# Modulation rows of a two-block network from four standing columns, two products per weight slice, folded afterwards

## The chip, the cores and the metric

The kernel runs on one core of a Trainium2 chip. The metric is the device time in microseconds (us) of the whole program; lower is better. Besides plain executions there is one profiled execution of the kernel before, and all durations below come from it.

## What is computed

The reference chains two networks of two layers each over 512 tokens of width 1024, all in float32. The part that the change touches is the modulation of the second network. Once per layer two vectors (one for the main tokens, one for the context tokens) are multiplied by a 1024 x 6144 matrix, a bias is added, and the two results are cut into six vectors of 1024 each: shift, scale and gate for the mixer, shift, scale and gate for the feed-forward part.

```python
silu_c = jax.nn.silu(c)
silu_cc = jax.nn.silu(c_ctx)
for i in range(DEPTH):                      # DEPTH = 2
    mod = (silu_c @ ada_w[i] + ada_b[i])[:, None, :]
    mod_c = (silu_cc @ ada_w[i] + ada_b[i])[None, None, :]
    sh_m, sc_m, g_m, sh_f, sc_f, g_f = jnp.split(mod, 6, axis=-1)
    shc_m, scc_m, gc_m, shc_f, scc_f, gc_f = jnp.split(mod_c, 6, axis=-1)
    h = modulate(rmsnorm(x, norm_mix_w[i]), sh_m, sc_m)
    ...
    x = x + g_m * y
    x = x + g_f * swiglu(modulate(rmsnorm(x, norm_ffn_w[i]), sh_f, sc_f), ...)
```

## The kernel before

The program is a chain of stages written by hand, each a block with a part for SyncE (SP, which issues the DMAs), ScalarE (ACT), VectorE (DVE) and TensorE (PE). The engines meet only at semaphores. A stage that begins with `join` waits on every engine for the last signals of the stage before, and also for the DMAs that the stage before registered with `loading`: those are waited for by each engine that joins.

Float32 precision in the large products comes from splitting both operands in two. A weight chunk of 1 MB (four slices of 128 x 512 floats) lands in one of the slots, ACT casts it to `w_hi` in two halves (`hi_until`, L244), DVE subtracts to get `w_lo` in two halves (`lo_until`, L254), and PE makes three products for each 128-row slice (`split_products`, L289 to L291): hi by hi, lo by hi, hi by lo. `w_hi` and `w_lo` have two buffers each, so the cast of chunk c waits until PE is done with chunk c-2 (`chunk_used`). In this stage the raw chunks have four slots, two in `raw` and two at the end of `arena`; SP issues the load of chunk c+4 when DVE has finished `w_lo` of chunk c (`stream`, L227).

`modulation` (L1467) has 24 chunks: twelve groups `g` of 512 output columns, with two chunks each. The stationary operand of PE is `pair`, the silu of the two vectors in hi and lo form, two columns each; the weights are the moving operand. After each group DVE adds the bias and writes two rows (`rows`, L1535). At the end SP stores both rows to `mod_rows` in DRAM (L1490), whose gate parts are broadcast back much later by `gate_tables`; PE turns the rows by 48 small transposes (L1523) into columns, DVE copies them to `modT` (L1538) and folds the norm weights in (L1543). The next stage, `mod_norm`, starts with a join on ACT (L465 in the first layer, L468 in the second). The last `hi_until` and `lo_until` also split the first chunk of that next stage, chunk number 24 counted from 0, before the last bias addition.

The two instances of the stage are called layer 0 and layer 1 below.

Of the kernel before, what the change touches and what calls it, by code (L numbers as in the profile page):

```python
# [19 lines left out]
F32 = mybir.dt.float32  # L20
F32R = mybir.dt.float32r
I32 = mybir.dt.int32
ALU = mybir.AluOpType
# [3 lines left out]
P = 128  # L27
D = 1024
# [14 lines left out]
KQ = 4  # L43
BANK = 512
# [76 lines left out]
def column_plan():  # L121

    names = [("mix_g0", 8), ("mix_g1", 8), ("xa_g0", 8), ("xa_g1", 8), ("mem_g0", 8), ("mem_g1", 8),
             ("ffn_g0", 8), ("ffn_g1", 8), ("ret_g", 4), ("hg_g", 4), ("lb", 12), ("odq", 1), ("odk", 1),
             ("xaq0", 2), ("xaq1", 2), ("xak0", 2), ("xak1", 2), ("cw0", 66), ("cw1", 66), ("cb0", 22),
             ("cb1", 22), ("nm0", 8), ("nm1", 8), ("nf0", 8), ("nf1", 8), ("c", 8), ("cc", 8),
             ("sgun", 4), ("decb", 4), ("ghn", 1)]
    plan, at = {}, 0
    for name, n in names:
        plan[name] = (at, n)  # L130
        at += n
    return plan, at


class Kernel:


    def __init__(self, nc, ctx, ins, out):
# [12 lines left out]
        self.w_lo = sb("w_lo", [P, 2, SLOT], F32R)  # L151
        self.arena = sb("arena", [P, ARENA])
        self.plan, ncol = column_plan()
        self.cols = sb("cols", [P, ncol])
        self.perms = sb("perms_sb", [P, 3 * P])
# [23 lines left out]
    def col(self, name, i=0, n=1):  # L179
        a = self.plan[name][0] + i  # L180
        return self.cols[:, a:a + n]
# [105 lines left out]
def split_products(pe, out, w, x, first, last):  # L287

    pe.matmul(out, w[0], x[0], start=first, stop=False)  # L289
    pe.matmul(out, w[0], x[1], start=False, stop=False)  # L290
    return pe.matmul(out, w[1], x[0], start=False, stop=last)  # L291
# [18 lines left out]
def stage_sems(k, stage, *names):  # L310

    k.entry = dict(k.latest)
    k.loads, k.begun = [x for x in k.loads if len(x[1]) < 4] + k.begun, []
    out = []
    for name in names:
        engine, what = name.split(":")
        key = f"{stage}_{what}" if engine == "dma" else f"{engine}_{what}"
        if key not in k.signals:
            k.signals[key] = Signal(k, engine, k.nc.alloc_semaphore(key))
        k.signals[key].base = k.signals[key].total  # L320
        out.append(k.signals[key])
    return out
# [1143 lines left out]

def modulation(k, W, l):  # L1467


    A = Arena(k)  # L1470
    rows, bias = A(6 * D), A(6 * D)
    sc = A(KD, 2)
    first = W[f"ada{l}"]
    n, nk = 6 * D // BANK, KD // KQ
    pair = [x[:, :, 0:2] for x in (k.hi, k.lo)]
    s_c_hi, s_c_lo, s_silu, s_bias, s_side, s_mm_done, s_freed, s_turned, s_modT, s_stored = stage_sems(k, f"ada{l}", "act:c_hi", "dve:c_lo", "act:silu", "dma:bias", "dma:side", "pe:mm_done", "dve:freed", "pe:turned", "dve:modT", "dma:stored")
    block = k.block
    for i in range(n * nk):
        k.chunk_used[first + i] = s_mm_done(i + 1)

    @block.sync
    def _(sp):
        k.join(sp, "pe", "dve", "act", "pool")
        b = k.ins["ada_b_2"]
        sp.dma_start(bias[0:2, :], bass.AP(b.tensor, b.offset + l * 6 * D, [[0, 2], [1, 6 * D]])).then_inc(*s_bias.up(16))
        if l == 0:
            sp.dma_start(k.X[:, TX:TALL, :], k.ins["ctx_2"][0].rearrange("(t p) d -> p t d", p=P)).then_inc(*s_side.up(16))
        k.stream(sp, first + n * nk)
        sp.wait_ge(*s_freed(n))
        sp.dma_start(k.mod_rows, rows[0:2, :]).then_inc(*s_stored.up(16))  # L1490
        k.loading(s_stored(16))
        sp.wait_ge(*s_stored(16))
        if l == 0:
            k.loading(s_side(16))

    @block.scalar
    def _(act):
        k.join(act, "pe", "dve", "act", "pool")
        for i, name in enumerate(("c", "cc")):
            act.activation(sc[:, :, i], k.col(name, 0, 8), ACT.Silu).then_inc(*s_silu.up(1))  # L1500
        act.wait_ge(*s_silu(2))
        act.copy(pair[0], sc).then_inc(*s_c_hi.up(1))
        for i in range(n * nk + 1):
            k.hi_until(act, first + i + 1)

    @block.tensor
    def _(pe):
        k.join(pe, "pe", "dve", "act", "pool")
        pe.wait_ge(*s_c_lo(1))
        for g in range(n):  # L1510
            if g >= 4:
                pe.wait_ge(*s_freed(g - 3))
            for q in range(nk):
                k.wait_split(pe, first + nk * g + q)
                w = k.split_chunk(first + nk * g + q)
                for kk in range(KQ):
                    ins = split_products(pe, k.ps[0:2, g % 4, :], [x[:, q * KQ + kk, :] for x in pair],
                                         [x[:, kk, :] for x in w], q == 0 and kk == 0,
                                         q == nk - 1 and kk == KQ - 1)
                ins.then_inc(*s_mm_done.up(1))  # L1520
        pe.wait_ge(*s_freed(n))
        for i in range(48):
            ins = pe.transpose(k.ps[:, 4, 2 * i:2 * i + 2], rows[0:2, i * P:(i + 1) * P], k.ident[0:2, 0:2])  # L1523
        ins.then_inc(*s_turned.up(1))

    @block.vector
    def _(dve):
        dve.wait_ge(*s_c_hi(1))
        dve.tensor_tensor(pair[1], sc, pair[0].bitcast(F32), ALU.subtract).then_inc(*s_c_lo.up(1))
        k.lo_until(dve, first + 2)  # L1530
        dve.wait_ge(*s_bias(16))
        for g in range(n):
            k.lo_until(dve, first + min(nk * g + 4, nk * n + 1))
            dve.wait_ge(*s_mm_done(nk * (g + 1)))
            dve.tensor_tensor(rows[0:2, g * BANK:(g + 1) * BANK], k.ps[0:2, g % 4, :],  # L1535
                              bias[0:2, g * BANK:(g + 1) * BANK], ALU.add).then_inc(*s_freed.up(1))
        dve.wait_ge(*s_turned(1))
        dve.tensor_copy(k.modT[:].rearrange("p a b -> p (a b)"), k.ps[:, 4, 0:96]).then_inc(*s_modT.up(1))  # L1538
        dve.wait_ge(*s_modT(1))
        for base, name in ((8, f"nm{l}"), (32, f"nf{l}")):  # L1540
            for i in range(2):
                m = k.modT[:, base:base + 8, i]
                dve.scalar_tensor_tensor(m, m, 1.0, k.col(name, 0, 8), ALU.add, ALU.mult).then_inc(*s_modT.up(1))  # L1543
        dve.wait_ge(*s_modT(5))


def mod_norm(k, name, tiles, which, end):
# [119 lines left out]

def ab_mixer(k, W):
    modulation(k, W, 0)
    mod_norm(k, "ab_norm", list(range(TALL)), 0, W["ab_u"])  # L1670
    A = Arena(k)
# [285 lines left out]

def cd_mixer(k, W):
    modulation(k, W, 1)
    mod_norm(k, "cd_norm", list(range(TALL)), 0, W["cd_f"])  # L1960
    A = Arena(k)
# [161 lines left out]
def pack_columns(inputs):  # L2123

    col = lambda a: np.ascontiguousarray(a, dtype=a.dtype).reshape(-1, P).T
    src = {"ret_g": inputs["ev_ret_norm_g"], "hg_g": inputs["ev_hg_norm_g"], "lb": inputs["hg_lb_logits"],
           "odq": inputs["od_q_norm_g"], "odk": inputs["od_k_norm_g"], "c": inputs["c_2"],
           "cc": inputs["c_ctx_2"], "sgun": inputs["ab_sgu_norm_w_2"], "ghn": inputs["cd_head_norm_w_2"],
           "decb": np.concatenate([inputs["cd_decay_b_fwd_2"], inputs["cd_decay_b_bwd_2"]], 1)}
    for l in range(2):  # L2130
        for name, key in (("mix_g", "mix_norm_g"), ("xa_g", "xa_norm_g"), ("mem_g", "xa_mem_norm_g"),
                          ("ffn_g", "ffn_norm_g"), ("xaq", "xa_q_norm_g"), ("xak", "xa_k_norm_g"),
                          ("cw", "ffn_conv_w"), ("cb", "ffn_conv_b"), ("nm", "norm_mix_w_2"),
                          ("nf", "norm_ffn_w_2")):
            src[f"{name}{l}"] = inputs[key][l]
    plan, n = column_plan()
    return np.concatenate([col(np.asarray(src[name])) for name in plan], 1)

# [38 lines left out]
```

## Time and profile before

| | value |
|---|---|
| median of 3 runs (lowest to highest) | 4140.07 us (4135.92 to 4140.22) |
| the profiled execution, its own time | 4140.34 us |
| its span in the trace | 4138.6 us |
| busy share PE, DVE, ACT, POOL | 86%, 42%, 30%, 1% |
| mean granted TensorE clock, share of full | 0.916 |
| modulation of layer 0 in the trace | from 2111.5 to about 2202.8 us |
| modulation of layer 1 in the trace | from 3269.9 to about 3356.6 us |

The busy shares are means over the whole program. The two modulation stages take some 178 us of it together, so a change inside them is read from those two stretches alone.

### The profile page before, as it was taken

The page shows a single profiled execution, that of the slowest core. Times are in us where ns is not written, and L with a number is a line of the kernel's source. Part 1 is how long each engine was busy: PE and PEld are TensorE (multiplying, and loading weights), DVE is VectorE, ACT ScalarE, POOL GpSimd, SP SyncE. Part 2 cuts the span into 40 slices and gives each one's busy share as a digit, 9 for nine tenths or more (in the row PEclk, how much of TensorE's full clock was granted, in tenths as well). Part 3 has the DMA queues.
Part 4 walks back from the last instruction along what each step waited for, and adds up shares of the span by engine and source line. Part 5 has one row for each costly group of instructions (what it writes and reads, how often), then busy time and mean ns, then how long its engine had stood idle before and what let it go on. Part 6 is the DMA issues. An engine that isn't in the chain of part 4 may idle for free. (4 is left out here: it accounts for less than half of the span.)

```text
span 4138.6 us, 39286 instructions
## 1 busy us (share of the span) xinstructions
PE 3546.6 (86%) x16452; PEld 2818.0 (68%) x16452; DVE 1747.7 (42%) x2354; ACT 1225.1 (30%) x1664; POOL 54.2 (1%) x40
## 2 busy tenths in 40 slices
PE   7786696899987787899988978799999889678998
PEld 5464585787874575688746856688878547467876
DVE  2447445444434535444454156431123561433234
ACT  3110243323333333322343124221122341223222
POOL 0003100000000000000000000000000000000000
PEclk9885798999998898999999989899999999679999
DMA  4120130232221022233263120222212441012322
GB/s 141 36 72 0 41 113 20 82 101 83 92 95 61 11 81 72 62 94 100 87 219 108 61 36 1 61 59 64 62 62 67 159 154 64 11 56 77 98 91 82
DMA packets 326817, 313.82 MB, mean 76 GB/s; under 512 B 22304, under 2 KB 250016, under 8 KB 326376
## 3 DMA queue, kind: packets, MB, share of 16 engines
q1 hardware_dynamic: 326640, 311.30, 24.2%
q8 instruction: 131, 2.15, 0.2%
q14 instruction: 46, 0.38, 0.0%
HBM read 309.06 MB, written 2.22 MB: 75 GB/s over the span
## 5 line engine op out<-in xcount | busy, mean ns | idle before, releaser
L289 PE MATMUL ps<-hT_hi,w_hi 128*128 128x512 f32 (+1 forms) x2640 | 968.0, 367 | 25.7 <-DVE arena L829 11.0
L290 PE MATMUL ps<-hT_lo,w_hi 128*128 128x512 f32 (+1 forms) x2640 | 965.9, 366 | 0.0
L291 PE MATMUL ps<-hT_hi,w_lo 128*128 128x512 f32 (+1 forms) x2640 | 965.1, 366 | 0.0
L254 DVE TENSOR_TENSOR w_lo<-raw,w_hi 128x1024 fp32r<-128x1024 f32 (+2 forms) x510 | 591.2, 1201 | 664.2 <-ACT w_hi L244 664.1
L289 PE MATMUL ps<-w_hi,hT_hi 128*128 128x512 f32 (+1 forms) x1768 | 703.8, 398 | 121.6 <-DVE hT_lo L726 77.7
L290 PE MATMUL ps<-w_lo,hT_hi 128*128 128x512 f32 (+1 forms) x1768 | 701.0, 396 | 0.0
L291 PE MATMUL ps<-w_hi,hT_lo 128*128 128x512 f32 (+1 forms) x1768 | 699.4, 396 | 0.0
L244 ACT CAST w_hi<-raw 128x1024 fp32r<-128x1024 f32 (+2 forms) x510 | 501.2, 1033 | 541.8 <-PE ps L291 529.3
L289 PEld LDWEIGHTS ps<-hT_hi,w_hi 128*128 128x128 f32 x2640 | 499.2, 189 | 112.6 <-issue 22.6
L291 PEld LDWEIGHTS ps<-hT_hi,w_lo 128*128 128x128 f32 x2640 | 498.7, 189 | 81.1
L290 PEld LDWEIGHTS ps<-hT_lo,w_hi 128*128 128x128 f32 x2640 | 499.3, 189 | 80.1
L289 PEld LDWEIGHTS ps<-w_hi,hT_hi 128*128 128x128 f32 (+1 forms) x1768 | 318.8, 180 | 234.2 <-issue 128.8
L291 PEld LDWEIGHTS ps<-w_hi,hT_lo 128*128 128x128 f32 (+1 forms) x1768 | 318.5, 180 | 93.9 <-issue 10.7
L290 PEld LDWEIGHTS ps<-w_lo,hT_hi 128*128 128x128 f32 (+1 forms) x1768 | 318.9, 180 | 85.8 <-issue 8.6
L726 DVE TENSOR_TENSOR hT_lo<-arena,hT_hi 128x2048 fp32r<-128x2048 f32 (+3 forms) x60 | 141.9, 2380 | 309.6 <-ACT hT_hi L701 309.6
L701 ACT CAST hT_hi<-arena 128x2048 fp32r<-128x2048 f32 (+3 forms) x60 | 117.7, 1978 | 360.0 <-PE ps L291 340.2
L2058 DVE TENSOR_TENSOR arena<-arena,ps 128x512 f32<-128x512 f32 x44 | 30.3, 688 | 456.7 <-ACT arena L2048 293.0
L526 PE MATMUL ps<-perms_sb,arena 128*128 128x128 f32 x400 | 71.8, 353 | 138.9 <-DVE arena L489 128.3
L539 ACT COPY arena<-ps 128x512 f32<-128x512 f32 (+2 forms) x87 | 46.6, 546 | 471.6 <-PE ps L291 421.5
L2046 ACT ACTIVATE arena<-ps 128x512 f32<-128x512 f32 x44 | 26.3, 598 | 484.0 <-PE ps L291 484.0
L526 PEld LDWEIGHTS ps<-perms_sb,arena 128*128 128x128 f32 x400 | 64.3, 187 | 146.6 <-DVE arena L489 131.4
L539 DVE COPY arena<-ps 128x512 f32<-128x512 f32 (+2 forms) x95 | 62.1, 662 | 214.2 <-PE ps L291 149.3
(225 smaller groups left out, 2713.5 us busy)
## 6 DMA issues: line engine op xcount, KB each, us to landing
raw<-in_ffn_w_in SPq DMA_DIRECT2D x88, 512.0 KB, 4.6
raw<-in_ada_w SPq DMA_DIRECT2D x24, 1024.0 KB, 5.2
arena<-in_ada_w SPq DMA_DIRECT2D x24, 1024.0 KB, 5.5
raw<-in_ffn_w_gate SPq DMA_DIRECT2D x44, 512.0 KB, 4.0
raw<-in_ffn_w_up SPq DMA_DIRECT2D x44, 512.0 KB, 5.3
raw<-in_ffn_w_out SPq DMA_DIRECT2D x20, 1024.0 KB, 5.0
raw<-in_ffn_w_down SPq DMA_DIRECT2D x20, 1024.0 KB, 5.1
raw<-in_ev_w_in SPq DMA_DIRECT2D x16, 1024.0 KB, 5.8
```

The lines of the kernel that those rows point to most:

```text
L244: act.copy(self.split_chunk(c)[0][:, half], self.raw_chunk(c)[:, half]).then_inc(self.split_hi, 1)
L254: ins = dve.tensor_tensor(lo[:, half], self.raw_chunk(c)[:, half], hi[:, half].bitcast(F32), ALU.subtract)
L289: pe.matmul(out, w[0], x[0], start=first, stop=False)
L290: pe.matmul(out, w[0], x[1], start=False, stop=False)
L291: return pe.matmul(out, w[1], x[0], start=False, stop=last)
L526: last = pe.transpose(k.ps[:, g % 8, i * P:(i + 1) * P], xn[:, t, kk * P:(kk + 1) * P], k.ident)
L539: return eng.tensor_copy(dst, src) if who == "dve" else eng.copy(dst, src)
L701: act.copy(k.hi[:, slot(q, 0):slot(q, 0) + size(q), 0:w_tok], y(q * KQ, size(q))).then_inc(*s_y_hi.up(1))
L726: dve.tensor_tensor(k.lo[:, r, 0:w_tok], y(q * KQ, size(q)), k.hi[:, r, 0:w_tok].bitcast(F32), ALU.subtract).then_inc(*s_y_lo.up(1))
L2046: ins = act.activation(sil[:, m % 2, 0:SEQ], k.ps[:, b0, :], ACT.Silu)
L2058: ins = dve.tensor_tensor(act_t[:, m, 0:SEQ], sil[:, m % 2, 0:SEQ], k.ps[:, b0 + 1, :], ALU.mult)
```

## The change

The four columns hi and lo of the two vectors now stand side by side in one stationary operand `quad` of four columns (in the hi buffer). Each weight slice gets two products, w_hi and w_lo, against all four columns, and gives four rows in PSUM: two from the hi columns and two from the lo columns. The product of lo by lo, absent before, is in the sum now. The bias buffer is four rows high, cleared by a memset of VectorE before SP loads the bias into its first two rows. The 48 transposes turn four rows, and VectorE adds the two halves in column form. The gate rows (2 x 2 x 512 columns) are folded from four rows to two by four products with a small 0/1 matrix `fold`, copied from PSUM by ScalarE to `gates`, and stored by two DMAs.

```diff
     A = Arena(k)
-    rows, bias = A(6 * D), A(6 * D)
+    rows, bias, gates = A(6 * D), A(6 * D), A(2 * D)
...
-    pair = [x[:, :, 0:2] for x in (k.hi, k.lo)]
+    quad = k.hi[:, :, 0:4]
+    fold = k.col("fold", 0, 2)[0:4]
+    gate_chunks = [4, 5, 10, 11]
...  sync
         b = k.ins["ada_b_2"]
+        sp.wait_ge(*s_clear(1))
         sp.dma_start(bias[0:2, :], bass.AP(b.tensor, b.offset + l * 6 * D, [[0, 2], [1, 6 * D]])).then_inc(*s_bias.up(16))
         if l == 0:
             sp.dma_start(k.X[:, TX:TALL, :], k.ins["ctx_2"][0].rearrange("(t p) d -> p t d", p=P)).then_inc(*s_side.up(16))
         k.stream(sp, first + n * nk)
-        sp.wait_ge(*s_freed(n))
-        sp.dma_start(k.mod_rows, rows[0:2, :]).then_inc(*s_stored.up(16))
-        k.loading(s_stored(16))
-        sp.wait_ge(*s_stored(16))
+        sp.wait_ge(*s_gates(4))
+        for i in range(2):
+            sp.dma_start(k.mod_rows[:, (2 + 3 * i) * D:(3 + 3 * i) * D],
+                         gates[0:2, i * D:(i + 1) * D]).then_inc(*s_stored.up(16))
+        k.loading(s_stored(32))
+        sp.wait_ge(*s_stored(32))
...  scalar
-        act.copy(pair[0], sc).then_inc(*s_c_hi.up(1))
+        act.copy(quad[:, :, 0:2], sc).then_inc(*s_c_hi.up(1))
         for i in range(n * nk + 1):
             k.hi_until(act, first + i + 1)
+        for i in range(4):
+            act.wait_ge(*s_folded(i + 1))
+            act.copy(gates[0:2, i * BANK:(i + 1) * BANK], k.ps[0:2, (5, 6, 7, 3)[i], :]).then_inc(*s_gates.up(1))
...  tensor
                 for kk in range(KQ):
-                    ins = split_products(pe, k.ps[0:2, g % 4, :], [x[:, q * KQ + kk, :] for x in pair],
-                                         [x[:, kk, :] for x in w], q == 0 and kk == 0,
-                                         q == nk - 1 and kk == KQ - 1)
+                    c4 = quad[:, q * KQ + kk, :]
+                    pe.matmul(k.ps[0:4, g % 4, :], c4, w[0][:, kk, :], start=q == 0 and kk == 0, stop=False)
+                    ins = pe.matmul(k.ps[0:4, g % 4, :], c4, w[1][:, kk, :], start=False,
+                                    stop=q == nk - 1 and kk == KQ - 1)
                 ins.then_inc(*s_mm_done.up(1))
         pe.wait_ge(*s_freed(n))
         for i in range(48):
-            ins = pe.transpose(k.ps[:, 4, 2 * i:2 * i + 2], rows[0:2, i * P:(i + 1) * P], k.ident[0:2, 0:2])
+            ins = pe.transpose(k.ps[:, 4, 4 * i:4 * i + 4], rows[0:4, i * P:(i + 1) * P], k.ident[0:4, 0:4])
         ins.then_inc(*s_turned.up(1))
+        for i, c in enumerate(gate_chunks):
+            pe.matmul(k.ps[0:2, (5, 6, 7, 3)[i], :], fold, rows[0:4, c * BANK:(c + 1) * BANK], start=True,
+                      stop=True).then_inc(*s_folded.up(1))
...  vector
+        k.join(dve, "pe", "dve", "act", "pool")
+        dve.memset(bias[0:4, :], 0.0).then_inc(*s_clear.up(1))
         dve.wait_ge(*s_c_hi(1))
-        dve.tensor_tensor(pair[1], sc, pair[0].bitcast(F32), ALU.subtract).then_inc(*s_c_lo.up(1))
+        dve.tensor_tensor(quad[:, :, 2:4], sc, quad[:, :, 0:2].bitcast(F32), ALU.subtract).then_inc(*s_c_lo.up(1))
...
-            dve.tensor_tensor(rows[0:2, g * BANK:(g + 1) * BANK], k.ps[0:2, g % 4, :],
-                              bias[0:2, g * BANK:(g + 1) * BANK], ALU.add).then_inc(*s_freed.up(1))
+            dve.tensor_tensor(rows[0:4, g * BANK:(g + 1) * BANK], k.ps[0:4, g % 4, :],
+                              bias[0:4, g * BANK:(g + 1) * BANK], ALU.add).then_inc(*s_freed.up(1))
         dve.wait_ge(*s_turned(1))
-        dve.tensor_copy(k.modT[:].rearrange("p a b -> p (a b)"), k.ps[:, 4, 0:96]).then_inc(*s_modT.up(1))
+        quads = k.ps[:, 4, 0:192].rearrange("p (a b) -> p a b", b=4)
+        dve.tensor_copy(k.modT[:], quads[:, :, 0:2]).then_inc(*s_modT.up(1))
         dve.wait_ge(*s_modT(1))
+        dve.tensor_tensor(k.modT[:], k.modT[:], quads[:, :, 2:4], ALU.add).then_inc(*s_modT.up(1))
```

The change moves instructions at the head and at the end of the stage. At the head of layer 0, VectorE's order of instructions (the names in brackets are the semaphores waited for; `arena` holds the bias buffer in the memset's row):

```order
-L1526 UNCONDITIONAL_BRANCH
-L1529 TENSOR_TENSOR hT_lo<-arena,hT_hi 128x8x2 [waits act_c_hi]
+L1539 UNCONDITIONAL_BRANCH
+L1542 MEMSET arena 4x6144 [waits act_sq,pool_key,dve_dve_freed,pe_used]
+L1544 TENSOR_TENSOR hT_hi<-arena,hT_hi 128x8x2 [waits act_c_hi]
 L254 TENSOR_TENSOR w_lo<-raw,w_hi 128x1024 [waits weights_split_hi] x2
 L254 TENSOR_TENSOR w_lo<-arena,w_hi 128x1024 [waits weights_split_hi,ada0_bias]
```

A memset of 6144 elements per partition has come in ahead of the lo half of the vectors, and the splitting of the second chunk stands behind it.

SyncE's order at the same place, from the end of the stage before to the first loads of this one:

```order
 L227 DMA raw<-in_ada_w 128x4x512 [waits weights_split_lo] x2
-L1481 UNCONDITIONAL_BRANCH
-L1485 DMA arena<-in_ada_b 2x6144 [waits pool_key,act_sq,odqn_loaded,dve_dve_freed,pe_used]
-L1487 DMA X<-in_ctx 128x2x1024
+L1484 UNCONDITIONAL_BRANCH
+L1489 DMA arena<-in_ada_b 2x6144 [waits pool_key,odqn_loaded,act_sq,dve_clear,dve_dve_freed,pe_used]
+L1491 DMA X<-in_ctx 128x2x1024
 L227 DMA arena<-in_ada_w 128x4x512 x2
 L227 DMA raw<-in_ada_w 128x4x512 [waits weights_split_lo] x2
```

The bias load has gained the wait for the memset (`dve_clear`), and the loads of the context and of chunks 2 to 5 are queued behind it on SP.

At the end of layer 0, ScalarE's order from the last cast of the stage to the first instruction of `mod_norm`:

```order
 L244 CAST w_hi<-raw 128x1024
+L1513 COPY arena<-ps 2x512 [waits pe_folded] x4
 L461 UNCONDITIONAL_BRANCH
-L465 ACTIVATE arena,stat<-X 128x1024 [waits pool_key,ada0_stored,act_c_hi,ada0_side,dve_modT,pe_turned]
+L465 ACTIVATE arena,stat<-X 128x1024 [waits pool_key,ada0_stored,act_gates,ada0_side,dve_modT,pe_folded]
 L465 ACTIVATE arena,stat<-X 128x1024 [waits act_sq]
```

Four copies have come in, and the first instruction of the next stage waits, as before, for the stored rows (`ada0_stored`). SyncE's order there:

```order
 L227 DMA raw<-in_ab_w_in 128x8x256 [waits weights_split_lo] x2
-L1490 DMA mod_rows<-arena 2x6144 [waits dve_freed]
+L1495 DMA mod_rows<-arena 2x1024 [waits act_gates]
+L1495 DMA mod_rows<-arena 2x1024
 L457 UNCONDITIONAL_BRANCH [waits ada0_stored]
```

The store went out when the rows were complete (`dve_freed`); now two smaller stores go out after ScalarE's four copies.

## Rows read from the trace of the kernel before

**Rows 1.** Stretches: engines' busy us, PE clock, DMA share, GB/s; layer 0, whole.

```profile
2111.00:2204.00 93.00, 74.55 (x336) 26.81 (x336) 64.58 (x66) 51.25 (x57) 0.00 (x0) 0.94 0.82 284
```

**Rows 2.** Waits from 2111 to 2204: who for whom, us, times, longest.

```profile
ACT w_hi L244 <- PE ps L291: 29.2, 21, 3.2
```

**Rows 3.** Timeline, one round of two chunks, layer 0 (start, duration us, instructions).

```profile
2181.47 2.00 ACT L244 CAST w_hi<-raw 128x1024 fp32r<-128x1024 f32 x2 [1.82 <-PE ps L291]
...
2182.55 2.36 DVE L254 TENSOR_TENSOR w_lo<-raw,w_hi 128x1024 fp32r<-128x1024 f32 x2 [0.87 <-ACT w_hi L244]
...
2185.06 0.39 PE L289 MATMUL ps<-w_hi,hT_hi 128*2 128x512 f32 x1 [0.91 <-DVE w_lo L254]
...
2187.60 0.67 DVE L1535 TENSOR_TENSOR arena<-ps,arena 2x512 f32<-2x512 f32 x1
...
2188.07 2.00 ACT L244 CAST w_hi<-arena 128x1024 fp32r<-128x1024 f32 x2 [1.82 <-PE ps L291]
```

**Rows 4.** Timeline of ACT: the casts of chunks 4 and 24 in each layer.

```profile
2128.73 1.99 ACT L244 CAST w_hi<-raw 128x1024 fp32r<-128x1024 f32 x2 [3.25 <-PE ps L291]
...
2194.69 1.99 ACT L244 CAST w_hi<-raw 128x1024 fp32r<-128x1024 f32 x2 [1.84 <-PE ps L291]
...
3282.62 2.00 ACT L244 CAST w_hi<-raw 128x1024 fp32r<-128x1024 f32 x2 [1.00 <-PE ps L291]
...
3348.55 2.00 ACT L244 CAST w_hi<-raw 128x1024 fp32r<-128x1024 f32 x2 [1.76 <-PE ps L291]
```

**Rows 5.** Stretches as in rows 1: transfers at the head, and in the steady part.

```profile
2120.00:2124.00 4.00, 1.05 (x5) 0.21 (x3) 2.07 (x2) 2.50 (x3) 0.00 (x0) 0.99 1.05 388
...
2160.40:2167.00 6.60, 5.70 (x25) 1.94 (x24) 5.32 (x6) 4.01 (x4) 0.00 (x0) 1.00 0.94 317
```

**Rows 6.** Timeline, heads of the two layers.

```profile
2111.54 0.26 SPq L1485 DMA_DIRECT2D arena<-in_ada_b  x1
...
2120.78 1.99 ACT L244 CAST w_hi<-arena 128x1024 fp32r<-128x1024 f32 x2 [5.48 <-DMA arena<-in_ada_w]
...
2124.34 0.59 PE L289 MATMUL ps<-w_hi,hT_hi 128*2 128x512 f32 x1 [3.29 <-DVE w_lo L254]
2124.73 0.63 PE L290 MATMUL ps<-w_lo,hT_hi 128*2 128x512 f32 x1
2125.16 0.63 PE L291 MATMUL ps<-w_hi,hT_lo 128*2 128x512 f32 x1
...
3276.02 2.00 ACT L244 CAST w_hi<-arena 128x1024 fp32r<-128x1024 f32 x2 [3.65 <-DMA arena<-in_ada_w]
```

**Rows 7.** Groups by form: the largest memset of VectorE.

```profile
L1655 DVE MEMSET scratch_sb<- 64x3072 f32 x1 | 2.6, 2618 | 0.8 <-DVE arena L1612 0.8
```

**Rows 8.** Timeline, end of layer 0, into the next stage.

```profile
2198.78 3.19 PE L1523 MATMUL ps<-perms_sb,arena 2*128 2x2 f32 x48 [1.40 <-DVE arena L1535]
...
2202.78 1.06 ACT L465 ACTIVATE arena<-X 128x1024 f32<-128x1024 f32 x1 [6.09 <-DVE modT L1543]
```

**Rows 9.** SyncE's own waits from 2110 to 2204.

```profile
SPq L457 <- DMA mod_rows<-arena: 2.7, 1, 2.7
```

**Rows 10.** The page's DMA issues: KB each, us from issue to landing.

```profile
arena<-in_colmask SPq DMA_DIRECT2D x1, 32.0 KB, 1.7
```

**Rows 11.** Stretches as in rows 1, across the end of the transposes of layer 0.

```profile
2200.40:2202.00 1.60, 1.57 (x25) 1.48 (x24) 0.00 (x0) 0.00 (x0) 0.00 (x0) 1.00 0.00 0
2202.00:2206.00 4.00, 0.00 (x0) 0.00 (x0) 0.66 (x5) 3.17 (x5) 0.00 (x0) 0.55 0.01 2
```

**Rows 12.** Groups by form: small float32 products, and ScalarE's copies from PSUM.

```profile
L1428 PE MATMUL ps<-arena 32*8 32x512 f32 x2 | 1.0, 584 | 1.4 <-DVE arena L539 1.4
...
L539 ACT COPY arena<-ps 128x512 f32<-128x512 f32 x70 | 40.2, 588 | 395.2 <-PE ps L291 346.1 <-PE ps L1727 26.3 <-PE ps L965 16.0
```

**Rows 13.** Stretches as in rows 1, in the attention and in an earlier decay stage.

```profile
2560.00:2570.00 10.00, 6.96 (x41) 4.90 (x40) 5.97 (x18) 4.73 (x16) 0.00 (x0) 1.00 0.00 0
340.00:350.00 10.00, 6.18 (x25) 5.29 (x25) 9.60 (x12) 0.00 (x0) 4.50 (x3) 0.50 0.01 2
```

More of the change, by code:

```diff
@@ L126, in column_plan @@
              ("cb1", 22), ("nm0", 8), ("nm1", 8), ("nf0", 8), ("nf1", 8), ("c", 8), ("cc", 8),
-             ("sgun", 4), ("decb", 4), ("ghn", 1)]
+             ("sgun", 4), ("decb", 4), ("ghn", 1), ("fold", 2)]
     plan, at = {}, 0
@@ L1474, in modulation @@
     n, nk = 6 * D // BANK, KD // KQ
-    pair = [x[:, :, 0:2] for x in (k.hi, k.lo)]
-    s_c_hi, s_c_lo, s_silu, s_bias, s_side, s_mm_done, s_freed, s_turned, s_modT, s_stored = stage_sems(k, f"ada{l}", "act:c_hi", "dve:c_lo", "act:silu", "dma:bias", "dma:side", "pe:mm_done", "dve:freed", "pe:turned", "dve:modT", "dma:stored")
+    quad = k.hi[:, :, 0:4]
+    fold = k.col("fold", 0, 2)[0:4]
+    gate_chunks = [4, 5, 10, 11]
+    s_c_hi, s_c_lo, s_silu, s_bias, s_side, s_mm_done, s_freed, s_turned, s_folded, s_modT, s_gates, s_clear, s_stored = stage_sems(
+        k, f"ada{l}", "act:c_hi", "dve:c_lo", "act:silu", "dma:bias", "dma:side", "pe:mm_done", "dve:freed", "pe:turned",
+        "pe:folded", "dve:modT", "act:gates", "dve:clear", "dma:stored")
     block = k.block
@@ L1534, in _ @@
             dve.wait_ge(*s_mm_done(nk * (g + 1)))
-            dve.tensor_tensor(rows[0:2, g * BANK:(g + 1) * BANK], k.ps[0:2, g % 4, :],
-                              bias[0:2, g * BANK:(g + 1) * BANK], ALU.add).then_inc(*s_freed.up(1))
+            dve.tensor_tensor(rows[0:4, g * BANK:(g + 1) * BANK], k.ps[0:4, g % 4, :],
+                              bias[0:4, g * BANK:(g + 1) * BANK], ALU.add).then_inc(*s_freed.up(1))
         dve.wait_ge(*s_turned(1))
-        dve.tensor_copy(k.modT[:].rearrange("p a b -> p (a b)"), k.ps[:, 4, 0:96]).then_inc(*s_modT.up(1))
+        quads = k.ps[:, 4, 0:192].rearrange("p (a b) -> p a b", b=4)
+        dve.tensor_copy(k.modT[:], quads[:, :, 0:2]).then_inc(*s_modT.up(1))
         dve.wait_ge(*s_modT(1))
+        dve.tensor_tensor(k.modT[:], k.modT[:], quads[:, :, 2:4], ALU.add).then_inc(*s_modT.up(1))
+        dve.wait_ge(*s_modT(2))
         for base, name in ((8, f"nm{l}"), (32, f"nf{l}")):
@@ L1543, in _ @@
                 dve.scalar_tensor_tensor(m, m, 1.0, k.col(name, 0, 8), ALU.add, ALU.mult).then_inc(*s_modT.up(1))
-        dve.wait_ge(*s_modT(5))
+        dve.wait_ge(*s_modT(6))
 def mod_norm(k, name, tiles, which, end):
@@ L2135, in pack_columns @@
             src[f"{name}{l}"] = inputs[key][l]
+    src["fold"] = np.tile(np.eye(2, dtype=np.float32), (P // 2, 1)).T
     plan, n = column_plan()
```

## The prediction

> **What bounds the kernel now.** The change touches two stretches, so the whole-program shares say little. I first took the stretch of layer 0 [rows 1]: TensorE is busy for 74.55 of 93.00 us, yet VectorE for 64.58 and the DMA engines for 0.82 of it. The reader is to see that nothing is full and three things are near it. Next the waits [rows 2]: the longest is ACT's cast waiting for PE, 29.2 us in 21 waits. That is the two-deep `w_hi`/`w_lo` ring: the cast of chunk c waits for the products of chunk c-2. The timeline [rows 3] gives one turn of that ring, two chunks: cast start 2181.47, first subtraction 2182.55 (+1.08, behind the first half of the cast), first product 2185.06 (+2.51), next cast 2188.07 (+3.01, twelve products and their tail). The sum is 6.60 us. The casts of chunks 4 and 24 [rows 4] lie 65.96 us apart in layer 0 and 65.93 in layer 1, ten turns each: 6.60 and 6.59. So the ring is what sets the pace throughout, and PE's products are 3.01 of its 6.60.
>
> Ahead of chunk 4 the pace is set by something else: ACT waited for the load of chunk 2 until 2120.78, 9.24 us after SP issued its first DMA at 2111.54 [rows 6]. Behind the last bias addition come the transposes, VectorE's short work on `modT`, and then ACT starts the next stage, 4.00 us after the first transpose [rows 8].
>
> **The change, part by part.**
>
> *Eight products for twelve.* In the steady part PE is busy 5.70 us with 25 products [rows 5], some 0.23 each. Four fewer take 0.92 from the 3.01: a turn is 1.08 + 2.51 + 2.09 = 5.68 us. Does something else take over? VectorE has two subtraction pairs of 2.36 and one addition of 0.67 in a turn [rows 3], 5.39 us, which is 0.29 less. (Four rows instead of two change neither the addition nor the copies, if the time goes by elements of a partition; rows 12 with 128 partitions and rows 3 with two are both at 0.6 to 0.7 us for 512 elements.) The transfers: two chunks are 2.10 MB, at the 388 GB/s of the head [rows 5] 5.40 us, 0.28 less than a turn. So both just fit, and the ten turns between the casts of chunks 4 and 24 save 10 x 0.92 = 9.2 us in each layer, **18.4 us** in all. If the transfers held only 350 GB/s, halfway from the 317 of the steady part to 388, a turn would be 5.99 and the two layers would save 12.2. Those are the ends: 12.2 and 18.4. I take 18.4, since 388 was held while the loads of the head were queued and a turn asks for 369.
>
> *The memset.* No memset of 6144 elements is in the trace; the nearest has 3072 on 64 partitions and takes 2.62 us [rows 7]. Twice the elements is 5.24 us, and I take 5.2. The lower end would be its share by partitions (4 of 64), about nothing. The Trainium skill ("VectorE: DVE Perf Modes", the section on zero memsets) says that a memset takes one cycle for each element whatever the type; with that page's clock this would be an estimate of 6.4 us, while the trace has 0.85 ns for each element. Going by the page adds 1.2 us to each head. Behind the memset waits SP with the bias, and behind that the context and chunks 2 to 5; also the lo half of the vectors, so PE's first product. Chunks 0 and 1 are already there, but cover nothing: what is late next is the load of chunk 2, and with it everything up to chunk 4. In layer 0 the cast of chunk 2 moves from 2120.78 to 2126.0, its products start 3.59 later (1.08 + 2.51), at 2129.6. PE comes to them from an idle time, as now: the products at 2124.73 and 2125.16 are 0.43 apart and last 0.63 [rows 6], the level of 1.2 GHz. From cast 2 to cast 4 it takes 7.95 us now [rows 4, 6], of it 4.4 behind the first product; four products of the warm kind fewer make 3.5. Cast 4 comes at 2133.1, **+4.3**. In layer 1, cast 2 moves from 3276.02 to 3281.2, products start at 3284.8. There PE found the full clock before (cast 2 to cast 4 in 6.60 [rows 4, 6]). It will not now: PE has eight products fewer to do and a load 5.2 later to wait for, an idle time longer than that before the slow ones of layer 0. So 3.5 again, cast 4 at 3288.3, **+5.7** (+4.3 if the clock stays up).
>
> *The end.* The 48 transposes take 3.19 us [rows 8], issued at one pace, and I leave them so with four columns. PE then folds: four float32 products of 512 columns. The nearest, two with 32 x 8 weights, take 584 ns each and 1.0 together [rows 12], so 0.43 apart. At the full clock the first copy of ACT starts at 3.19 + 0.6 = 3.8 and four copies of 0.59 [rows 12] end at 6.2. The clock is 1.00 in the transposes and 0.55 right behind them [rows 11], so it falls within half a microsecond of the time at which the folds begin. With three of four folds at 1.2 GHz (0.86 apart) the last ends at about 6.7 and its copy at 7.3. The Trainium skill ("TensorE: Matmul & The Clock Gate", part 4) says that transposes don't count as busy PE for the clock; the trace agrees as far as it goes, with this fall. Then SP issues two stores, 0.4 us, and each engine's join waits for them. The one store now was waited for 2.7 us behind its issue [rows 9], which was hidden behind transposes and `modT`. A load of 32 KB lands in 1.7 [rows 10]; I take 1.9 for 8 KB, between the two. So the next stage starts at 7.3 + 0.4 + 1.9 = 9.6 and not 4.0. I take 9.4, **+5.4 in each layer, 10.8** (ends: 8.3, all at full clock and 1.7, +4.3; 10.4, 2.7 to land, +6.4). VectorE's extra addition on 96 columns, under 0.3, lies beside the folds and costs nothing; without them it would cost 0.3.
>
> *At nothing.* The bias loads wait behind the memset but VectorE needs the bias only after chunk 3. The gates are read back hundreds of us later. SP's next loads were issued before the stores. Two more columns in `cols` are 1 KB in a load.
>
> *The sum.* -18.4 + 4.3 + 5.7 + 10.8 = **+2.4 us**. On the profiled execution's own time that is 4142.7; it lies 0.3 above the median, so on the median 4142.5. The ends of the costs: heads 8.6 and tails 8.6 against 18.4 give -1.2; 12.2 saved, heads 10.0 and tails 12.8 give +10.6.
>
> **The rivals.** A measurement of this kernel tells about 0.2%, 8.3 us, from no change.
>
> *The transfers pace the loop* (slower). For it: the DMA share is 0.94 at 317 GB/s [rows 5], and the rate of 388 appears only where the cast, the subtraction and the products are mostly waiting. Against it: there, at a share of 1.05, it was held for chunk after chunk at the head. With turns of 5.99, the middle heads and tails, the sum is -12.2 + 20.8 = +8.6, 4148.7; it decides from a turn of about 5.98 us on. With a rate of 340 it is 4152.
>
> *The clock falls in the loop* (slower). PE would have eight products in each 2.84 us, busy about 70%, with idle times of nearly 1 us between the chunks. The decay stage sits at 0.50 with PE busy 6.18 of 10 us, the attention at 1.00 with 6.96 [rows 13]; the loop would be at the second. If it fell, eight products take 0.20 x 7 + 0.23 more, the turn is 5.68 + 1.6 = 7.3, and each layer loses 7 us in the loop where it was to gain 9.2: -18.4 + 18.4 + 14 + 21 = some +35, 4175. The Trainium skill ("TensorE: Matmul & The Clock Gate", on clock oscillation in real kernels) speaks for this: short bursts with waits between let the clock drop again at each burst. Its waits are longer than these, and no stretch here with such short ones shows it.
>
> *The memset is short or hidden* (faster). If its time went by the partitions too, the heads would have no delay and would save the four products (0.9 each): -18.4 - 1.8 + 10.8 = -9.4, 4130.7. Against it: the row of 2.62 us.
>
> *The stores aren't waited for on the path.* Then the tails are 2.2 to 3.3 each, the sum is -3, 4137: no change that can be told. Against it: the order shows `ada0_stored` in the first wait of ACT.
>
> **How the numbers follow.** Forecast, within 0.2%: 0.56, and the case of the stores 0.08 lands there too, with 0.04 of the transfers' case: same 0.68. Slower: transfers or several ends high 0.17, clock 0.07: 0.24. Faster: 0.08. The range from 4136 to 4152 takes in the forecast with its bounds, the stores' case and most of the transfers' case, and leaves the clock and the short memset out.
>
> **What would show it.** Right: casts of chunks 4 and 24 about 57 us apart; first DMA of the stage 5.2 us later than the last square of ACT; folds partly 0.86 apart; ACT's first instruction of the next stage some 9.4 us behind the first transpose. Wrong: casts 60 us or more apart with ACT waiting for DMA (transfers), products 0.43 apart in the steady part (clock), a memset below 3 us, or ACT starting before the stores have landed.

## The result, and the profile after

The changed kernel takes 4160.57 us (median of 6 runs, 4152.21 to 4165.89) against 4140.6 us (6 runs, 4135.92 to 4145.19) timed beside it: ratio 1.0044, 95% interval 1.0029 to 1.0059, **20 us or 0.44% slower**. The forecast was 4142.5 with a range from 4136 to 4152. Timed again later beside new runs of the kernel before, four runs gave 4161.98 against 4141.98, ratio 1.0044, interval 1.0031 to 1.0058.

Stretches of the changed kernel's profiled execution (the columns are those of [rows 1]): the steady part of the loop in layer 0, then the transposes and the folds behind it.

```profile
2153.00:2193.00 40.00, 28.33 (x114) 8.58 (x112) 36.73 (x36) 27.96 (x28) 0.00 (x0) 1.00 1.02 365
2197.30:2202.30 5.00, 5.00 (x48) 5.00 (x48) 0.00 (x0) 0.00 (x0) 0.00 (x0) 0.53 0.00 0
2202.30:2209.30 7.00, 7.00 (x9) 0.84 (x9) 0.91 (x6) 1.72 (x3) 0.00 (x0) 0.50 0.00 0
```

The loop runs at the full clock with the transfers at 365 GB/s. The transposes run at a granted clock of 0.53 and the folds at 0.50, the lower of the two levels; before, the clock was still 1.00 in the transposes [rows 11].

The timeline of ACT, casts of chunks 4 and 24 in each layer, which answer to [rows 4] (the first row merges the casts of chunks 4 and 5; its start is that of chunk 4):

```profile
2136.49 3.89 ACT L244 CAST w_hi<-raw 128x1024 fp32r<-128x1024 f32 x4 [2.41 <-PE ps L1528]
...
2193.22 2.00 ACT L244 CAST w_hi<-raw 128x1024 fp32r<-128x1024 f32 x2 [1.51 <-PE ps L1528]
...
3305.60 1.99 ACT L244 CAST w_hi<-raw 128x1024 fp32r<-128x1024 f32 x2 [2.53 <-PE ps L1528]
...
3362.35 2.00 ACT L244 CAST w_hi<-raw 128x1024 fp32r<-128x1024 f32 x2 [1.51 <-PE ps L1528]
```

They are 56.73 and 56.75 us apart, where it was 65.96 and 65.93. The loop's gain is 9.2 us in each layer, as worked out.

The head of layer 0 in the timeline, which answers to [rows 6] and [rows 7]:

```profile
2113.19 0.19 ACT L710 ACTIVATION_READ_ACCUMULATOR scratch_sb<-X 128x1 f32 x1
...
2114.88 5.18 DVE L1542 MEMSET arena<- 4x6144 f32 x1 [4.61 <-issue]
...
2120.16 0.26 SPq L1489 DMA_DIRECT2D arena<-in_ada_b  x1
...
2129.38 1.99 ACT L244 CAST w_hi<-arena 128x1024 fp32r<-128x1024 f32 x2 [12.12 <-DMA arena<-in_ada_w]
```

The memset lasts 5.18 us, and starts 1.5 us after ACT's last work of the stage before (2113.38), the moment called the join from here on. SP's first DMA comes 6.8 us after that moment, where it was 0.1.

The end of layer 0, which answers to [rows 8], and of layer 1:

```profile
2197.30 5.10 PE L1533 MATMUL ps<-perms_sb,arena 4*128 4x4 f32 x48 [2.00 <-DVE arena L1550]
2202.33 6.98 PE L1536 MATMUL ps<-arena,cols 4*2 4x512 f32 x8
...
2204.23 0.57 ACT L1513 COPY arena<-ps 2x512 f32<-2x512 f32 x1 [9.02 <-PE ps L1536]
...
2209.35 0.57 ACT L1513 COPY arena<-ps 2x512 f32<-2x512 f32 x1 [1.13 <-PE ps L1536]
2211.80 1.06 ACT L465 ACTIVATE arena<-X 128x1024 f32<-128x1024 f32 x1 [1.88 <-DMA mod_rows<-arena]
...
3366.44 3.91 PE L1533 MATMUL ps<-perms_sb,arena 4*128 4x4 f32 x48 [1.99 <-DVE arena L1550]
...
3379.65 1.28 ACT L468 ACT_TABLE_LOAD   x1 [1.78 <-DMA mod_rows<-arena]
```

ACT's four copies come 1.71 us apart (2204.23 to 2209.35 is three such steps), one behind each fold. Four folds make **eight** records, 6.98 us, in layer 1 the same. From the first transpose to the next stage it is 14.50 us in layer 0 and 13.21 in layer 1; it was 4.00 and 3.99 [rows 8 for layer 0].

To see where the whole difference lies I cut every profile at the same places: the end of ACT's last work before the stage, ACT's first instruction behind it, and in between the two layers ACT's first copy of the window attention and its first cast of the projection behind that attention. Lengths in us, worked out from the starts in the timelines of ACT:

| kernel (profiled execution) | layer 0 | layer 1 | both against before | window attention | median against that of before, timed beside it |
|---|---|---|---|---|---|
| before | 91.36 | 86.85 | | 150.77 | |
| before, second profile | 91.34 | 87.16 | | 150.76 | |
| changed | 98.42 | 94.26 | +14.5 | 157.61 | +20.0 |
| changed, second profile | 97.87 | 93.62 | +13.3 | 150.72 | (one run, +11.8) |
| changed, third profile | 98.40 | 94.65 | +14.8 | 157.46 | +20.0 |

Against the first profile of before, the changed kernel's first profile is 23.3 us longer in span: 14.5 in the two stages, 6.8 in the window attention, which the change doesn't touch, and 2.0 ahead of layer 0. Each of the three stretches left agrees within 0.4. The time ahead of layer 0, in which no kernel here has an edit, runs from 2106.9 to 2116.5 us over all thirteen profiles. So the end of one profile can't be compared with the end of another to better than some 10 us; the stages can.

### The profile page after: what moved, and what is told of

It reads as the page before. It is cut to its first block and busy times, and to the rows that moved or that the text cites. A ratio compares the mean times of both kernels' runs of the same rounds, so it can differ in the third digit from the quotient of the medians.

```text
span 4161.9 us, 38954 instructions
## 1 busy us (share of the span) xinstructions
PE 3536.1 (85%) x16276; PEld 2814.1 (68%) x16276; DVE 1756.5 (42%) x2358; ACT 1229.0 (30%) x1672; POOL 54.2 (1%) x40
## 5 line engine op out<-in xcount | busy, mean ns | idle before, releaser
L289 PE MATMUL ps<-w_hi,hT_hi 128*128 128x512 f32 x1576 | 626.8, 398 | 82.1 <-DVE hT_lo L726 77.7
L290 PE MATMUL ps<-w_lo,hT_hi 128*128 128x512 f32 x1576 | 623.8, 396 | 0.0
L291 PE MATMUL ps<-w_hi,hT_lo 128*128 128x512 f32 x1576 | 622.6, 395 | 0.0
L289 PEld LDWEIGHTS ps<-w_hi,hT_hi 128*128 128x128 f32 x1576 | 302.6, 192 | 151.6 <-issue 82.6
L291 PEld LDWEIGHTS ps<-w_hi,hT_lo 128*128 128x128 f32 x1576 | 302.3, 192 | 64.3
L290 PEld LDWEIGHTS ps<-w_lo,hT_hi 128*128 128x128 f32 x1576 | 302.9, 192 | 62.8
```

## The experiments

**The memset alone**, added to the kernel before.

```diff
+        sp.wait_ge(*s_clear(1))
         sp.dma_start(bias[0:2, :], ...)
...
+        k.join(dve, "pe", "dve", "act", "pool")
+        dve.memset(bias[0:4, :], 0.0).then_inc(*s_clear.up(1))
         dve.wait_ge(*s_c_hi(1))
```

> The kernel before with one part of the change: VectorE clears four bias rows of 6144 elements at the head of each modulation, and SyncE waits for it ahead of the bias load and all that is queued behind. Theory: in the changed kernel the memset starts 1.5 us after the join and lasts 5.18, so loads start 6.7 us late; twelve products stay, and in layer 1 the clock has fallen when chunk 2 comes (+1.4). So +6.7 and +8.1, about 4155 us against 4140.6. Rival, the memset's delay is covered (chunks 0 and 1 have already landed) and the changed kernel's loss is all at the end of the stage: 4141.

Measured: 4165.25 us (4158.0 to 4171.11, 4 runs) against 4140.66 (22 runs), ratio 1.0057, interval 1.0039 to 1.0076. Layer 0 takes 99.51 and layer 1 93.41, together +14.7 against before; +14.8 was expected. The memset is on the path with its late start; the rival falls. That the sum came out so near is luck: by layer it is +8.2 and +6.6, where +6.7 and +8.1 were expected. The heads cost +6.5 and +6.6, and the other 1.7 lie at the end of layer 0, where the 48 transposes, the same as before, took 4.87 us at a granted clock of 0.56 in place of 3.19 at 1.00. The median is another 10 us longer than the two stages account for.

**The zeros by a DMA**, changed kernel without memset.

```diff
-        sp.wait_ge(*s_clear(1))
         sp.dma_start(bias[0:2, :], ...).then_inc(*s_bias.up(16))
+        sp.dma_start(bias[2:4, :], k.ins["zrow"]).then_inc(*s_bias.up(16))
...
-        k.join(dve, "pe", "dve", "act", "pool")
-        dve.memset(bias[0:4, :], 0.0).then_inc(*s_clear.up(1))
```

> The changed kernel without the memset and its wait: the two rows of zeros come by a DMA of 48 KB from a constant. Theory: heads go from +5.8 and +7.4 (measured in the changed kernel's trace) to -0.9 + 0.3 each, the loop keeps its -9.2 in each layer, the ends keep +10.5 and +9.2: 0 in all, 4141 us. Rival, that the attention stage behind layer 0 is 6 us longer because of the change (it was 6.2 us longer in the changed kernel's profile): 4147.

Measured: 4151.17 us (7 runs), ratio 1.0026, interval 1.0015 to 1.0037. Stages 92.09 and 90.40, together +4.3 against before, 10.2 less than in the changed kernel. The expectation was 0: in layer 0 the cast of chunk 2 comes 10.8 us behind the join instead of 9.4, in layer 1 8.1 instead of 6.2, and its eight products run in the low clock, so the heads cost +0.7 and +2.4 where -0.6 each was expected. All three kernels with the zero rows have chunk 2 late by 1.1 to 2.2 us; the added DMA stands ahead of its load on SP, and no run tests it apart from the rest. The median is 10 us above the 4141 expected, with a window attention of 159.46 us in the profile.

**No folds**, changed kernel.

```diff
-        sp.wait_ge(*s_gates(4))
-        for i in range(2):
-            sp.dma_start(k.mod_rows[:, ...], gates[0:2, i * D:(i + 1) * D])...
+        sp.wait_ge(*s_freed(n))
+        sp.dma_start(k.mod_rows, rows[0:2, :]).then_inc(*s_stored.up(16))
...
-        for i in range(4):
-            act.wait_ge(*s_folded(i + 1))
-            act.copy(gates[0:2, ...], k.ps[0:2, (5, 6, 7, 3)[i], :])...
...
-        for i, c in enumerate(gate_chunks):
-            pe.matmul(k.ps[0:2, (5, 6, 7, 3)[i], :], fold, rows[0:4, ...], ...)
```

> The changed kernel without the four fold products and ScalarE's copies; the rows from the hi columns alone are stored when complete, as in the kernel before (the part of the gates that comes from the lo columns of the vectors is left out). Theory: the ends keep only the slower transposes (5.10 and 3.91 us instead of 3.19) and the extra addition, about +3 for both layers; heads +5.8 and +7.4, loop -18.4: -2, 4139 us. Rival, the store's landing and not the folds is what the end waits for: then the ends stay at more than +4 each, 4147 or more.

This kernel leaves out the part of the gates that comes from the lo columns. Measured: 4142.79 us (10 runs), ratio 1.0001, interval 0.9991 to 1.0010. Stages 89.11 and 86.39, together -2.7 against before and 17.2 less than in the changed kernel; the theory had -2. The median is 2 us above before's, with a window attention of 153.28 us in the profile. The store of the rows, 2.7 us behind its issue as before, is hidden again, so the folds, the copies and the store queued behind them are what the end paid for, and not the landing by itself.

**The products alone**: both edits together, with the same part of the gates left out.

> Both at once: eight products instead of twelve, zeros by DMA, no folds (gates without the lo columns' part). What is left of the change is the loop's gain. Theory: loop -18.4, heads -1.2, ends +3: -16.6, 4124 us. Rival (a longer attention stage comes with the change): 4130.

Measured: 4128.89 us (4123.41 to 4140.56, 10 runs), ratio 0.9973, interval 0.9964 to 0.9983. Stages 83.27 and 82.84, together -12.1. What the eight products give is there, and less than the 16.6 expected: the heads cost +0.4 and +2.5 in place of -0.6 each, for chunk 2 comes later and its products run in the low clock, the ends cost +0.7 and +1.0, and the loop of layer 1 gained only 7.5. There the casts of chunks 4 and 24 are 58.44 us apart and not 56.7, because three casts of the loop waited for their loads, the longest (at 3336.20) for 2.23 us. The profiled execution, with a window attention of 157.97 us, took 4140.56, the slowest of the ten.

**The folds in the loop**, changed kernel with memset: three folds behind the products of groups 6, 7 and 11, ACT's copies between its casts, the last fold ahead of the transposes.

```diff
                 ins.then_inc(*s_mm_done.up(1))
+            if g in (6, 7, 11):
+                fold_gate((6, 7, 11).index(g))
+        fold_gate(3)
         for i in range(48):
             ins = pe.transpose(...)
...  scalar
             k.hi_until(act, first + i + 1)
+            if i in (15, 17, 24):
+                take_gate((15, 17, 24).index(i))
+        take_gate(3)
```

> The changed kernel with the four folds moved: three into the loop, behind the products of groups 6, 7 and 11, where PE idles 1.7 us in each turn, with ScalarE's copies between its casts; the last fold ahead of the transposes. Theory (what costs at the end is the folds' and copies' place, behind the transposes and ahead of the store): one fold, 48 transposes and modT, about 6.5 us from the last bias addition to the next stage instead of 4.0, so +2.5 each instead of +10.5 and +9.2; heads as in the changed kernel: both stages together +1 against before, 4142 to 4148. Rival, the folds at 1.2 GHz in the loop push the ring: the loop's gain shrinks by 2 us or more in each layer.

Measured: 4145.29 us (4136.08 to 4156.73, 10 runs), ratio 1.0010, interval 1.0001 to 1.0020. Stages 89.61 and 88.02, together -0.6 against before and 15.1 less than the changed kernel. From the join to the cast of chunk 24 it is 80.03 and 77.20 us, 0.2 more than in the changed kernel, so the folds in the loop cost next to nothing. The group by form shows the price of a fold at the full clock (16 records are the eight folds of both layers; mean ns of one record):

```profile
L1527 PE MATMUL ps<-arena,cols 4*2 4x512 f32 x16 | 8.1, 587 | 1.8 <-DVE arena L1562 1.8
```

Busy 8.1 us, where the same eight products take 14.0 in the changed kernel: 1.0 each alone at the full clock, 1.75 behind the transposes. The ends cost +1.5 and +2.7, for the transposes still meet the fall of the clock (3.45 and 4.70 us). In layer 0 three casts of the loop waited for their loads here too, 1.2 us at most. The median stands 3.7 us higher against before than the stages do.

**Everything hidden**: zeros by DMA, folds in the loop, the 32 transposes whose columns are read moved into the loop, the 16 of the gates left out since nothing reads them, and the stores' landing waited for one stage later.

```diff
+            if g >= 2 and g - 2 not in gate_chunks:
+                pe.wait_ge(*s_freed(g - 1))
+                for i in range(4 * (g - 2), 4 * (g - 1)):
+                    ins = pe.transpose(...)
...
-        k.loading(s_stored(32))
+        k.rows_stored = s_stored(32)
... mod_norm
     norm_transpose(k, name, tiles, at(o + 8), at(o), end)
+    if which == 0:
+        k.loading(k.rows_stored)
```

> Zeros by DMA, folds in the loop as before, the 32 transposes that are used moved into the loop too (those of the gates are left out, nothing reads them), and the stores of the gates waited for one stage later. The whole result is computed. Theory: loop -18.4, heads -1.2, ends about 1.5 us shorter than before each: -22.8 in the two stages, 4118 us, up to 6 more if the attention stage is in its longer form. Rival, the work in the loop isn't free (ACT's copies and PE's transposes delay casts and products of the ring): 4128.

Measured: 4126.21 us (4120.5 to 4129.31, 5 runs) against 4142.18 (15 runs), **ratio 0.9960**, interval 0.9947 to 0.9972: faster than both kernels. Stages 81.15 and 78.69, together -18.4; -22.8 was expected. The part missing is mostly at the heads, +0.9 and +2.5 in place of -0.6 each, and 1.1 us in the loops (57.09 and 57.53), where chunk 12 in layer 0 and chunk 13 in layer 1 waited 1.7 us for their loads; the ends gave 2.2 each, more than expected. The end of layer 0, timeline of ACT:

```profile
2182.76 2.00 ACT L245 CAST w_hi<-raw 128x1024 fp32r<-128x1024 f32 x2 [1.48 <-PE ps L1542]
...
2188.64 1.06 ACT L466 ACTIVATE arena<-X 128x1024 f32<-128x1024 f32 x1 [0.16 <-ACT arena L1508]
```

The next stage starts 0.2 us behind the last copy and 5.9 behind the start of the last cast; in the kernel before that was 8.1 and in the changed one 18.6.

**The same kernels once more**, for second profiles.

> The kernel before once more, for a second profile of it. If the longer attention stage (157.6 us in the changed kernel's profile, 150.8 in that of before) belongs to the change, this shows 151 us again; if it differs from one execution to the next, it can be anywhere between 150 and 160.

> The changed kernel once more, for a second profile: the modulation stages must be again 98.4 and 94.3 us; the attention stage tells, with the run of the kernel before, whether its length is a matter of the kernel or of the execution.

Measured: 4142.44 and 4154.01 us, one run each. The window attention took 150.76 us in the kernel before and 150.72 in the changed one. So the changed program can run it in the short form, and the longer one doesn't come with every execution.

**A plain delay in the kernel before**, of dead work at the end of each modulation.

```diff
         dve.wait_ge(*s_modT(5))
+        dve.memset(bias[0:4, 0:6144], 0.0).then_inc(*s_modT.up(1))   # 2048 elements in the other kernel
+        dve.wait_ge(*s_modT(6))
```

> The kernel before, with a plain delay at the end of each modulation: VectorE clears 6144 dead elements (5.2 us) before the next stage may start. Nothing else differs. Theory A (the extra time outside the two stages comes from when the attention is reached, not from what the change does): the stages grow by 5.3 each, 10.6, and the median by more than that, 4153 to 4158, with runs spread over more than 10 us. Theory B (it comes from something else in the change): 4141.5 + 10.6 = 4152, spread as before (some 10 us).

> As the run with 5.2 us, but 2048 elements (1.8 us by 0.83 ns each). Theory A: stages +1.9 each, 3.8, and the median up to 6 more: 4146 to 4151. Theory B: 4145.3.

> The changed kernel again, timed beside them on one chip, with a third profile. The modulation stages 98 and 94 us again; the median 4155 to 4163, and the attention stage anywhere from 150.7 to 159.

Measured: 5.2 us of delay, 4155.65 us (6 runs), ratio 1.0032, interval 1.0021 to 1.0044; 1.8 us of delay, 4155.38 us (6 runs), ratio 1.0031, interval 1.0019 to 1.0043. A third of the delay costs about the same, 13.7 and 13.4 us. The stages grew by +16.2 (97.91 and 96.50) and by +4.9 (93.69 and 89.46), where 10.6 and 3.8 were expected. Of the excess in the first, 2.7 us are the late start of the two memsets, 2.0 the head of layer 1 and 1.1 slower transposes there. The changed kernel timed beside them is the one told above as the third profile: its median of 4161.98 is inside the 4155 to 4163 expected.

The memsets of the two delays (the kernel with 5.2 us, then that with 1.8):

```profile
2201.07 5.18 DVE L1545 MEMSET arena<- 4x6144 f32 x1 [1.33 <-issue]
```

```profile
2202.63 1.76 DVE L1545 MEMSET arena<- 4x2048 f32 x1 [0.48 <-DVE modT L1543]
```

The window attention as one stretch, in this order: before, 1.8 us of delay, changed kernel, changed kernel in its second profile (columns as in [rows 1]); with 5.2 us of delay it took 150.75:

```profile
2443.07:2593.84 150.77, 129.83 (x834) 101.33 (x834) 88.94 (x217) 69.95 (x177) 0.00 (x0) 0.98 0.00 1
```

```profile
2444.83:2603.00 158.17, 140.80 (x834) 109.34 (x834) 89.59 (x217) 69.85 (x177) 0.00 (x0) 0.90 0.00 1
```

```profile
2451.99:2609.60 157.61, 138.88 (x834) 108.10 (x834) 89.25 (x217) 69.94 (x176) 0.00 (x0) 0.92 0.00 1
```

```profile
2449.84:2600.56 150.72, 128.91 (x834) 101.38 (x834) 88.90 (x217) 69.95 (x175) 0.00 (x0) 0.98 0.00 1
```

The same 834 product records, VectorE and ScalarE busy for the same time within 0.7 us, and a mean clock of 0.98 in the short ones and 0.90 to 0.92 in the long ones. The difference sits late in the stretch. From 112 to 135 us behind its start, before and then with 1.8 us of delay:

```profile
2555.07:2578.07 23.00, 17.89 (x122) 14.19 (x122) 12.79 (x43) 10.48 (x35) 0.00 (x0) 1.00 0.00 1
```

```profile
2556.83:2579.83 23.00, 21.34 (x87) 17.41 (x86) 9.49 (x30) 7.47 (x26) 0.00 (x0) 0.56 0.00 1
```

The kernel with 1.8 us of delay differs from before by nothing but that delay. Its median is 8.5 us above what its stages add, and both theories had less (4146 to 4151, and 4145.3). So theory B falls: time outside the two stages is lost without anything of the change. That it is lost in the attention rests on one profile of that kernel (+7.4 there). With 5.2 us of delay the profile had the short form and the median was 2.5 below what the stages of that profile add, so A's claim that any shift brings the excess falls too.

Nor is it the moment at which the attention starts. It started at 2449.84 and at 2449.77 us in two profiles of the changed kernel and took 150.72 and 157.46; at 2444.77 before and at 2444.83 with 1.8 us of delay it took 150.76 and 158.16. What does go with the length is how far behind the start of the stretch the granted clock first falls:

| first fall, us behind the start | stretch, us | profiles |
|---|---|---|
| 0.7 and 0.9 | 153.1 and 153.3 | memset alone; no folds |
| 1.25 | 159.5 | zeros by a DMA |
| 1.6 | 157.5 and 157.6 | changed kernel, two of three |
| 1.7 to 2.0 | 150.7 to 150.9 | before, both; changed kernel, second; 5.2 us of delay; everything hidden |
| 2.8 and 2.9 | 158.2 and 158.0 | 1.8 us of delay; products alone |
| none in the first 119 | 152.0 | folds in the loop |

The changed kernel stands in two of these lines. This is seen and not tested: no run moves the fall alone.

## Why the prediction was wrong

*What bounds the kernel, and the loop.* Right. A turn of 5.68 was forecast and 5.67 was measured (56.73 / 10), 18.4 us in both layers. Transfers: 365 GB/s with ACT waiting for PE throughout, as the stretch and the casts' brackets show; that rival falls for the changed kernel, whose three profiles have 56.65 to 56.75 us in the loop. The margin is as thin as the forecast had it: in three kernels built from it (products alone, folds in the loop, everything hidden) single casts did wait for loads, and the loop took 57.0 to 58.4 us in four of their six layers. Clock in the loop: 1.00; that rival falls too, with PE busy 28.33 of 40 us. What the Trainium skill ("TensorE: Matmul & The Clock Gate", on clock oscillation in real kernels) tells of clocks that drop again between bursts did not happen in this loop, with idle times of about 1 us.

*The memset.* Right in its place on the path, too small in its price. From the join to the cast of chunk 4 it is now 23.1 and 20.2 us where it was 17.3 and 12.8: +5.8 and +7.4, forecast +4.3 and +5.7. The part behind the load is as forecast (cast of chunk 2 to cast of chunk 4 in 7.11 and 7.23 us, forecast 7.09). What is short is the 5.2: the row does last 5.18 us, but it starts 1.5 us late (2114.88 against 2113.38), in all four kernels that have this memset. The late start grows with the size of the memset. Where only VectorE's own work stood ahead of it, the idle time before the row is 0.05 us for 512 elements, 0.48 for 2048, 0.75 for 3072 and 1.33 for 6144. Idle time and row together are 1.05 to 1.10 ns for each element throughout, 6.5 us for 6144. So the row's duration alone is no price for a memset, and [rows 7] had 0.8 us of idle time printed beside its 2.6. The prediction's other estimate, 6.4 us and 1.2 more for each head, was the nearer one. Whether the engine already clears in that idle time, no run shows.

*The end: the step that failed.* "The nearest, two with 32 x 8 weights, take 584 ns each and 1.0 together, so 0.43 apart." That row [rows 12] has x2, but the program has that product **once** on that line: a float32 product of 512 columns leaves two records in the trace. The row said 1.0 us for one product, and the prediction priced a fold at half of it. Another group of the kernel before could have told: 32 such products back to back at the full clock, in 64 records.

```profile
L1727 PE MATMUL ps<-arena 128*128 128x512 f32 x64 | 27.7, 593 | 1.4 <-DVE arena L539 1.4
```

That is 0.86 us for a product, and 1.71 with the clock at its lower level. The four folds lasted 6.98 us where the forecast has about 3.5 (6.7 - 3.19). "Folds partly 0.86 apart" stood among the signs of being right, and the records are indeed 0.85 apart; but each is half a fold. The transposes add to it: 5.10 and 3.91 us, forecast 3.19, at a granted clock of 0.53 and 0.74. "Issued at one pace" held only as long as the clock did; the slow transposes don't come from the eight products, for they are there with the memset alone too (4.87 us). The last copy ended 12.6 us behind the first transpose in layer 0, forecast 7.3. From there, with the issue and the landing of the stores, it was 1.9 us to the next stage, less than the 2.3 taken. The prediction's terms add up to 9.6 for the whole, and it took 9.4 without a reason. Measured are 14.50 and 13.21, that is +10.5 and +9.2 at the ends, against +5.4 each. The path was right (folds, copies, stores, join), and the experiment without folds, -17.2 us in the two stages, shows it.

By these terms the sum is -18.4 + 5.8 + 7.4 + 10.5 + 9.2 = +14.5, 12 above the forecast of +2.4. Of the miss, 9 lie at the ends and 3 at the heads.

*Outside the change: the step that wasn't there.* The remaining 5 to 6 us of the median are not in the two stages. The prediction took it that a stage that isn't edited keeps its time. The window attention runs in 150.7 to 159.5 us by how much of it gets the low clock. It took over 157 in two of three profiles of the changed kernel, in none of two of the kernel before, and in three other kernels (1.8 us of delay, zeros by a DMA, products alone). Against what the stages add, the medians of the eight experiments lie from 2.5 below to 9.9 above.

That the long form alone makes up the difference of the medians is an inference from profiles: three profiles don't give how often it comes. Nor is it settled why 11 to 22 runs of before stay within 11 us while some of the other kernels spread over up to 21; no run here fixes where the attention starts against the clock's changes.

## What to carry to other kernels

Before a row's duration is used as the price of a new instruction, compare its count with the number of instructions of that line in the program: here a float32 product of 512 columns had two, and each was half of it. Look at the idle time printed before a row too, as the memset shows. Work that a change adds ahead of a loop or behind it, in a chain across engines (PE, ACT, a store, a join), was paid in full: the loop gave 18.4 us here and the heads and ends took 33 back, while the whole result computed with the folds and the used transposes in the loop's idle time, the zeros by a DMA and the stores waited for later made the kernel 16 us faster than before. And where an untouched stage changes its time with the clock, a difference under 10 us is read by stages from several profiles, not from medians.

## What had not been expected of the hardware

A plain float32 product of 512 columns costs 0.86 us from start to start at the full clock (32 products in 27.7 us) and 1.71 at the lower level (the folds, with weights of 4 x 2), and each leaves two records. A memset's row on VectorE starts late by an idle time that grows with its size, 0.05 us at 512 elements and 1.33 at 6144. The transposes behind the loop took 3.19 us at the full clock and up to 5.10 where the clock fell in them. And an untouched stage of 150.7 us took up to 8.7 us more, and its length went with where the granted clock first fell in it.
